# A hybrid encoder step: its input projection computed by Strassen's seven products

## What is computed

```python
h = rmsnorm(x, norm_g)
proj = jnp.einsum('btd,de->bte', h, w_in)      # (tokens, 1024) x (1024, 3592)
pu, pg, q, k, v, ag, fl, cb, cc, cx, cgate = jnp.split(proj, _split_points(), axis=-1)
# pool branch: trailing means of pu minus pu, times pool_w, gated by silu(pg)
q = rmsnorm(q.reshape(B, T, N_ATT_HEADS, HEAD_DIM), q_norm_g)
k = rmsnorm(k.reshape(B, T, N_ATT_HEADS, HEAD_DIM), k_norm_g)
logf = jax.nn.log_sigmoid(fl + b_f)            # forgetting attention over q, k, v, logf, gated by silu(ag)
z = cc * cx                                    # conv branch: cb * causal conv of width 3 of z, gated by silu(cgate)
x_out = x + jnp.einsum('bte,ed->btd', mixed, w_out)
```

## Time and profile before

| | us |
|---|---|
| median of 3 runs | 1608.34 |
| lowest and highest | 1605.97, 1609.19 |
| the profiled execution | 1604.41 |
| its span | 1602.6 |
| first product of the input projection | 18.32 |
| prompt attention's first transposes | 747.13 |

### The profile page before, as it was taken

One profiled execution on the slowest core, in us unless ns is written; L12 is line 12 of the kernel. 1 busy time (PEld: TensorE's weight loads), 2 busy tenths in 40 slices (PEclk: granted clock), 3 DMA queues, 4 the chain that ended last, 5 costly groups with the idle time before them and its releaser, 6 DMA issues.

```text
span 1602.6 us, 24609 instructions
## 1 busy us (share of the span) xinstructions
PE 1536.1 (96%) x9264; PEld 1355.1 (85%) x9264; DVE 821.8 (51%) x2069; ACT 631.3 (39%) x1347; POOL 410.6 (26%) x706
## 2 busy tenths in 40 slices
PE   6999999999999899999999999999998999899999
PEld 5998888878799899898888888888887778688887
DVE  3333112232444422214988988888896788832221
ACT  4443121121211201113877877877975444410100
POOL 1110005555400000022444444444423355200000
PEclk9999999999999899999999999999999999899999
DMA  5433122121110200422133233233233665634441
GB/s 150 149 108 100 42 87 76 47 92 53 62 51 20 70 19 11 85 44 49 36 76 64 58 69 71 49 67 72 49 116 113 222 217 184 238 109 141 129 148 66
DMA packets 181511, 144.63 MB, mean 90 GB/s; under 512 B 104016, under 2 KB 140785, under 8 KB 181393
## 3 DMA queue, kind: packets, MB, share of 16 engines
q1 hardware_dynamic: 178880, 134.08, 28.8%
q10 hardware_dynamic: 2448, 8.91, 1.4%
q0 software_dynamic: 64, 0.07, 0.1%
HBM read 106.50 MB, written 36.53 MB: 89 GB/s over the span
## 4 chain that ended last, share of the span: by engine, by line
PE 52%; DVE 6%; ACT 4%; DMA 2%; issue 2%; POOL 1%; SPq 0%; ACTq 0%; POOLq 0%
PE banks L2263 12%; PE banks L920 12%; PE banks L1546 6%; PE banks L1537 4%; PE banks L1532 3%; PE banks L1562 3%; PE banks L1563 3%; DVE sa_v_lo L1920 2%; PE banks L2021 2%; PE banks L2002 2%; PE banks L1515 2%; ACT pa_s_ring L1386 1%; ACT pa_pt_hi L1415 1%; DMA pa_q_raw<-scratch_q 1%; PE banks L2051 1%
## 5 line engine op out<-in xcount | busy, mean ns | idle before, releaser
L914 PE MATMUL banks<-in_w_hi,in_xt_hi 128*128 128x512 f32 (+1 forms) x680 | 242.4, 356 | 4.6 <-DVE in_w_lo L644 3.1
L914 PE MATMUL banks<-in_w_hi,in_xt_lo 128*128 128x512 f32 (+1 forms) x680 | 239.6, 352 | 0.0
L914 PE MATMUL banks<-in_w_lo,in_xt_hi 128*128 128x512 f32 (+1 forms) x680 | 238.7, 351 | 0.0
L1436 DVE CUSTOM_DVE_ANT_0 pa_s_ring<-banks,pa_f_b 128x512 f32<-128x512 f32 (+2 forms) x320 | 193.2, 604 | 35.8 <-PE banks L1537 33.1
L920 PE MATMUL banks<-in_xt_hi,in_w_hi 128*128 128x384 f32 (+1 forms) x576 | 196.7, 342 | 8.2 <-DVE in_w_lo L644 8.0
L1484 DVE TENSOR_TENSOR pa_pt_lo<-banks,pa_pt_hi 128x512 fp32r<-128x512 f32 (+2 forms) x320 | 193.0, 606 | 21.3 <-ACT pa_pt_hi L1415 18.7
L920 PE MATMUL banks<-in_xt_hi,in_w_lo 128*128 128x384 f32 (+1 forms) x576 | 191.9, 333 | 0.0
L920 PE MATMUL banks<-in_xt_lo,in_w_hi 128*128 128x384 f32 (+1 forms) x576 | 191.8, 333 | 0.0
L1415 ACT ACTIVATE pa_pt_hi<-banks 128x512 fp32r<-128x512 f32 (+2 forms) x320 | 166.6, 534 | 54.1 <-PE banks L1546 52.9
L1546 PE MATMUL banks<-ident,pa_s_ring 128*128 128x128 f32 x1088 | 174.0, 275 | 9.7 <-DVE pa_pt_lo L1484 4.2
L1562 PE MATMUL banks<-pa_pt_hi,pa_vs 128*128 128x256 f32 x576 | 163.6, 300 | 0.4 <-DVE pa_parts L1464 0.3
(11 more groups left out here) (245 smaller groups left out, 2810.8 us busy)
## 6 DMA issues: line engine op xcount, KB each, us to landing
sa_k_c<-in_cache_k_dram SPq DMA_DIRECT2D x8, 2048.0 KB, 9.8
sa_v_c<-in_cache_v_dram SPq DMA_DIRECT2D x8, 2048.0 KB, 8.2
in_w_raw<-in_w_in_dram SPq DMA_DIRECT2D x48, 256.0 KB, 3.7
out_dram<-in_out SPq DMA_DIRECT2D x34, 256.0 KB, 2.0
out_dram<-op_y ACTq DMA_DIRECT2D x17, 512.0 KB, 5.1
in_x<-in_x_prompt_dram SPq DMA_DIRECT2D x16, 512.0 KB, 3.5
op_x<-in_x_prompt_dram SPq DMA_DIRECT2D x16, 512.0 KB, 4.9
pa_f_b<-scratch_f SPq DMA_DIRECT2D x28, 256.0 KB, 5.2
```

Of the source, the lines that this page charges most:

```text
L914: mm = pe.matmul(ps[:, u % NBANK, 0:n], tile_of(xa, t)[:, k, :], wa[:, k, c0:c0 + n], start=(k == 0 and q == 0), stop=(k == KT - 1 and q = ...
L1436: done = dve.tensor_tensor_reduce(scores_of(j)[:, b * P:(b + nb) * P], ps_s[:, (h * NQD + at) % 3, 0:nb * P], f_b[h % 2][:, b * P:(b + nb) ...
```

## The change

The input projection is computed by one level of Strassen's scheme in Winograd's form. Operand x is a pair of token tiles (A1., A2.) with the model's depth in halves (A.1, A.2); operand w has its depth in halves and each phase's columns in halves. Eight block products become seven, each of 4 k x 3 matmuls:

| no. | x operand | w operand |
|---|---|---|
| 0 | A11 | B11 |
| 1 | S2 = S1 - A11 | T2 = B22 - T1 |
| 2 | S1 = A21 + A22 | T1 = B12 - B11 |
| 3 | S3 = S2 - A22 | T3 = B12 - B22 |
| 4 | A12 | B21 |
| 5 | S4 = A12 - S2 | B22 |
| 6 | A22 | T4 = B21 - T2 |

The norm's gain goes to x, in one pass of DVE (SCALAR_TENSOR_TENSOR with g_b in SBUF), not to w. ACT copies product 0 out of PSUM (`copy_first`, L811); DVE adds product 1 (`make_u`, L1200), product 2 (`make_v`, L1206) and the rest to the four quarters (C22 L1221, C12 L1229, C21 L1257; C11 by ACT, L831 or L857, from bank 0, where product 4 is accumulated on product 0). Products 0 to 3 have a PSUM bank each, products 4, 5, 6 go to banks 0, 2, 3.

The 17 tiles go in three blocks: 3, 3 and 2 pairs, and the sample tile in the third, computed without Strassen from the same w operands (`sample`, L1569 and L1572, 48 matmuls a phase for rows). A "work" is one pair in one phase (channels: one of two column halves, over all tokens of a half block). ITEMS gives the order of phases; where one phase's block is followed by the same phase's, the weights stay. There are 19 sets ("gens") of weights. Each has a top and a bottom buffer (8 loads of 256 KB, for CONV0 and CONV1 16 of half that, issued when the former set's last low half is made), four sums T1 to T4 on POOL (`add_weights`, L609 to L617), seven high halves on ACT (L804) and seven low halves on DVE (L1033), all in single buffers. ACT may write the high half n when the last work of the former set has done product n, and product n of the first work waits for the low half n.

The x sums are DVE's (L1005 to L1026), their low halves POOL's (`split_sums`, L624), the other low halves DVE's (L984), the high ones ACT's (L791). Rows of KEY and QRY go to SBUF first: squares by ACT (L880), reduce by DVE (L1041), scale by POOL (`qk_scale`, L632 and L636), multiply by DVE (L1049), gain by DVE for the second tile (L1056) and by POOL for the first (L642). The pool branch and the convolution are in blocks of 768 or 512 tokens. Prompt attention waits for the same events under new names.

The core of the diff (by_rows and by_channels of before; of after the order, SP's load, POOL's steps, ACT's and DVE's, the product and PE's loop):

```diff
-def by_rows(u, t, k, c0, n):
-    for q, (xa, wa) in enumerate(((xt_hi, w_hi), (xt_hi, w_lo), (xt_lo, w_hi))):
-        mm = pe.matmul(ps[:, u % NBANK, 0:n], tile_of(xa, t)[:, k, :], wa[:, k, c0:c0 + n],
-                       start=(k == 0 and q == 0), stop=(k == KT - 1 and q == 2))
-    return mm
...
-def by_channels(u, c, k, c0):
-    for q, (wa, xa) in enumerate(((w_hi, xt_hi), (w_hi, xt_lo), (w_lo, xt_hi))):
-        mm = pe.matmul(ps[:, u % NBANK, 0:chunk_tokens(c)], wa[:, k, c0:c0 + P], xa[c][:, k, :],
-                       start=(k == 0 and q == 0), stop=(k == KT - 1 and q == 2))
-    return mm
...
+HALF = (3, 3, 2)
+BASE = (0, 6, 12)
+NBLK = 3
+ITEMS = ([(0, ph) for ph in (GATE, KEY, QRY, POOL, CONV0, CONV1, VAL)]
+         + [(1, ph) for ph in (VAL, KEY, QRY, POOL, CONV0, CONV1, GATE)]
+         + [(2, ph) for ph in (GATE, VAL, KEY, QRY, POOL, CONV0, CONV1)])
+A11_B11, S2_T2, S1_T1, S3_T3, A12_B21, S4_B22, A22_T4 = range(7)
+BANK = (0, 1, 2, 3, 0, 2, 3)
...
+def w_source(ph, n):
+    wd = width(ph)
+    return (quarter(ph, 0, 0), t2[:, :, 0:wd], t1[:, :, 0:wd], quarter(ph, 0, 1), quarter(ph, 1, 0),
+            quarter(ph, 1, 1), t4[:, :, 0:wd])[n]
...
+def load_w(gen):
+    ph = gens[gen]
+    if gen:
+        sp.wait_ge(w_lo_done, 7 * gen)
+    for top, dst, sem in ((0, w_top, top_in), (4, w_bot, bot_in)):
...
+def add_weights(gen, n):
+    ph = gens[gen]
+    wd = width(ph)
+    if n == 0:
+        pool.wait_ge(top_in, loaded(gen))
+        pool.wait_ge(bot_in, loaded(gen))
+        pool.tensor_tensor(t1[:, :, 0:wd], quarter(ph, 0, 1), quarter(ph, 0, 0), ALU.subtract).then_inc(t_made, 1)
+    elif n == 1:
+        pool.wait_ge(t_made, 4 * gen + 1)
+        pool.tensor_tensor(t2[:, :, 0:wd], quarter(ph, 1, 1), t1[:, :, 0:wd], ALU.subtract).then_inc(t_made, 1)
+    elif n == 2:
+        pool.tensor_tensor(quarter(ph, 0, 1), quarter(ph, 0, 1), quarter(ph, 1, 1), ALU.subtract).then_inc(t_made, 1)
+    else:
+        pool.wait_ge(t_made, 4 * gen + 2)
+        pool.tensor_tensor(t4[:, :, 0:wd], quarter(ph, 1, 0), t2[:, :, 0:wd], ALU.subtract).then_inc(t_made, 1)
+def split_sums(f):
+    b, i = FORMS[f]
+    dst = x_op[slot_of(b, i)]
+    for n, (op, tmp) in enumerate(((S1_T1, 0), (S4_B22, 2), (S3_T3, 1))):
+        pool.wait_ge(xh_done, before(f, 7, 3) + (4, 5, 7)[n])
+        pool.tensor_tensor(dst[:, op, 1, :, :].rearrange("p k n -> p (k n)"), s_tmp[tmp][:, :],
+                           dst[:, op, 0, :, :].rearrange("p k n -> p (k n)").bitcast(F32),
+                           ALU.subtract).then_inc(xs_done, 1)
+def qk_scale(w, a):
+    n = qk_count(w, a)
+    at = a
+    pool.wait_ge(qk_ss, n + 1)
+    pool.tensor_scalar(h_ms[:, at, :], h_ss[:, at, :], 1.0 / HD, EPS, ALU.mult, ALU.add).then_inc(qk_rs, 1)
+    pool.wait_ge(qk_rs, 2 * n + 1)
+    if qk_count(w, 0):
+        pool.wait_ge(qk_mul, qk_count(w, 0))
+    pool.tensor_tensor(h_rstd[:, at, :], h_ms[:, at, :], neg_half[:, :], ALU.pow).then_inc(qk_rs, 1)
...
+x_scale(0)
+x_scale(1)
+pool.memset(pw[:, :, :], 0.0).then_inc(made, 1)
+pool.wait_ge(t_made, 2)
+add_weights(0, 2)
+split_sums(0)
+add_weights(0, 3)
+x_scale(2)
+x_scale(3)
...
+if prev and prev.phase in (KEY, QRY):
+    for a in range(len(tiles(prev))):
+        qk_scale(prev, a)
+if w.phase in (KEY, QRY) and w.makes:
+    add_weights(w.gen + 1, 2)
+    add_weights(w.gen + 1, 3)
...
+if w.last and w.phase in (CONV0, CONV1):
+    mult_z(w.block, w.phase - CONV0)
+gen = w.gen + 1
+if ITEMS[w.item][1] != ITEMS[min(w.item + 1, len(ITEMS) - 1)][1]:
+    if w.index == 1:
+        add_weights(gen, 0)
+        add_weights(gen, 1)
+    if w.last and w.phase not in (KEY, QRY):
+        add_weights(gen, 2)
+        add_weights(gen, 3)
...
+def high_w(gen, n):
...
+if gen:
+    last = [w for w in works if w.gen == gen - 1][-1]
+    act.wait_ge(proj, done(last, n))
+act.activation(w_half(ph, n, 0), w_source(ph, n), ACT.Copy).then_inc(w_hi_done, 1)
...
+square_x(0)
+high_x(0, 0)
+square_x(1)
+keep_x(0)
+high_w(0, 0)
+for n in range(1, 7):
+    high_x(0, n)
+    high_w(0, n)
+square_x(2)
+square_x(3)
...
+if w.strassen:
+    copy_first(w)
+if here == (2, CONV1, 3):
+    after_work(1)
+if prev and prev.makes:
+    high_w(prev.gen + 1, 5)
+    high_w(prev.gen + 1, 6)
...
+if w.makes:
+    high_w(w.gen + 1, 0)
...
+if prev:
+    finish(prev)
+if w.makes:
+    high_w(w.gen + 1, 1)
+    high_w(w.gen + 1, 2)
...
+c11(w)
...
+if w.makes:
+    high_w(w.gen + 1, 3)
+    high_w(w.gen + 1, 4)
...
+def low_w(gen, n):
+    ph = gens[gen]
+    dve.wait_ge(w_hi_done, 7 * gen + n + 1)
+    dve.tensor_tensor(w_half(ph, n, 1), w_source(ph, n), w_half(ph, n, 0).bitcast(F32),
+                      ALU.subtract).then_inc(w_lo_done, 1)
...
+def make_u(w):
+    n = tokens(w.block) if w.phase >= POOL else width(w.phase)
+    dve.wait_ge(proj, done(w, S2_T2))
+    dve.wait_ge(s1_done, w.pairs + 1)
+    if w.pairs:
+        dve.wait_ge(c21_done, w.pairs)
+    dve.tensor_tensor(u2[:, 0:n], ps[:, 1, 0:n], sv[:, 0:n], ALU.add).then_inc(u_done, 1)
+def make_v(w):
+    n = tokens(w.block) if w.phase >= POOL else width(w.phase)
+    dve.wait_ge(proj, done(w, S1_T1))
+    dve.wait_ge(u_done, w.pairs + 1)
+    dve.tensor_tensor(sv[:, 0:n], ps[:, 2, 0:n], u2[:, 0:n], ALU.add).then_inc(v_done, 1)
...
+def product(w, n):
+    b, ph = w.block, w.phase
+    if n == A11_B11 and w.n:
+        pe.wait_ge(c11_done, w.n)
+    elif n == S2_T2 and w.pairs:
+        pe.wait_ge(u_done, w.pairs)
+    elif n == S1_T1 and w.n:
+        pe.wait_ge(c12_done, w.n)
+    elif n == S3_T3 and w.pairs:
+        pe.wait_ge(c21_done, w.pairs)
+    elif n == A12_B21:
+        pe.wait_ge(s1_done, w.pairs + 1)
+    elif n == S4_B22:
+        pe.wait_ge(v_done, w.pairs + 1)
+    elif n == A22_T4:
+        pe.wait_ge(c22_done, w.pairs + 1)
+    if w.fresh:
+        pe.wait_ge(w_lo_done, 7 * w.gen + n + 1)
+    if ITEMS.index((b, ph)) == 7 * b:
+        wait_x(w, n)
+    for k in range(4):
+        for q, (xh, wh) in enumerate(((0, 0), (0, 1), (1, 0))):
+            opens, closes = OPENS[n] and k == 0 and q == 0, k == 3 and q == 2
+            if ph < POOL:
+                mm = pe.matmul(ps[:, BANK[n], 0:width(ph)], x_op[slot_of(b, w.at)][:, n, xh, k, :],
+                               w_op[n][:, wh, k, 0:width(ph)], start=opens, stop=closes,
+                               skip_group_check=not OPENS[n])
+            else:
...
+pe.wait_ge(made, 2)
+turn_x(0)
+for w in works:
+    aside(w, -1)
+    for n in range(7 if w.strassen else 2):
+        if w.strassen:
+            product(w, n)
+        else:
+            sample(w, n)
+        aside(w, n)
```

2071 lines of the change are left out of this document (1253 added, 818 removed).

## The result

The changed kernel takes **1711.8 us** (median of 4 runs, 1708.9 to 1714.7), the kernel before 1607.2 (1605.6 to 1609.2). The ratio is 1.0651, with a 95% interval of 1.0634 to 1.0669: slower by 105 us. Forecast were 1664 and a range of 1587 to 1710.

What follows compares the result with a forecast made beforehand. PE was taken to bound the input projection. From 1604.4 us: products -66.7, start +22.4, old gaps -25.2, switches +57, +40, +8, x +10, clock +10, sum +55.5, giving 1659.9; plus 3.9 for the median, 1664 (range 1587 to 1710).

Steps and rivals of the forecast that it cites:

- Start and gaps of before: Input projection: first product near 42.4 us, +22.4 us; the old kernel's idle and clock losses go, -25.2 us.
- Products: PE in the input projection: 4680 short matmuls become 3768 longer ones, priced by width, -66.7 us.
- Contention: Weight switches: DVE subtractions and POOL sums, both reading SBUF, run nearly one after the other, 2.5 to 4 us a switch.
- the walk: KEY to QRY switch followed through POOL's queue: T3, T4 and their halves late, about 7 us without contention.
- The clock: PE goes to half clock after waits at the 18 switches, 3.4 us lost each time, three times: +10 us.
- x formed beside products: Eight works that form x operands beside their products, some 10.5 us of DVE in 9.95: 1.2 each, +10 us.
- six out of KEY or QRY: Six weight switches out of KEY or QRY: late T3, T4 and halves plus contention, 9.5 us each, +57 us.
- eight out of POOL, CONV0, CONV1: Eight weight switches out of the channel phases: late loads and sums plus contention, 5 us each, +40 us.
- four others: Four switches between GATE, VAL and KEY, with no scales in POOL's queue: 2 us each, +8 us.
- The rival of the powers: POOL's 34 powers (1.64 us each) also block DVE: 42 us more, 1706; 0.16 together with the clock rival.
- The rival of the clock at every switch: PE's clock falls at each of 18 switches: 56 us in place of 10, 1710; 0.16 together with the powers.
- Faster: Switches nearly covered, stalls and clock in the stage under 69.5 us: mostly 1570 to 1601 us; chance 0.26.

Runs made afterwards that it cites:

- e9: Changed kernel with each POOL weight sum replaced by three fills that only write, about 2.45 us (values wrong): 1660.5 us, ratio 1.0332.
- e5: Changed kernel plus 24 unread 256-column matmuls put into PE's waits, twice at each of four switches (KEY to QRY, QRY to POOL, first two blocks): 1708.3 us, ratio 1.0632.
- e1: Changed kernel with all weight sets after the first left out (loads, sums, halves and the products' waits for them): 1568.2 us, ratio 0.9755.
- e8: Changed kernel with second pair's transposes behind product 3 of the first work, and DVE instead of POOL making T3, T4 at all 18 switches: 1661.6 us, ratio 1.0349.
- e11: As e8, and DVE also makes T1 and T2 where the next set is formed in GATE, VAL, KEY or QRY works: 1636.7 us, ratio 1.0192.
- e2: Changed kernel with POOL's four sums of every weight set after the first replaced by fills of 8 columns (values wrong): 1611.3 us, ratio 1.0028.
- e10: Changed kernel with all but 8 columns of DVE's seven low halves left out in every weight set after the first: 1647.7 us, ratio 1.0252.

## Why the prediction was wrong

**Its direction and its mechanism held, its size did not.** The range was missed by 1.8 us, the centre by 48.

- *Start and gaps of before*: right, 42.22 for 42.4. *Products*: 8.7 us too good by the price of N=128.
- *What ends the waits*: right as a chain, wrong as a label. The prediction said 100 us or more would be ended by L1033; it is 18 of 108, and DVE's additions end 66. L1033 at a mean of 1.5 to 1.8 us was right (1.64). The waits were said to be longest at products 3 to 6 after KEY and QRY; those at product 3 are there (3.79, 4.46 and 4.00 us), but the longest are 9.34 and 6.68, at product 5 of the last POOL work.
- *Contention*: right in mechanism and about right in size, 43 against e9's 51. One of its readings was off: by the rows shown, the four subtractions and the multiply, 4.1 us of work, took 3.77, not 3.94.
- **The step that failed is the cost of a switch: the walk, which gave no loss to the last work ahead of it, and "The clock": "three times, +10" beside it.** PE idles for 108 us against 115 forecast, but the lower clock takes 60 more. The two can't be added as separate prices, though. e5 shows it: with the clock up the waits grow. What was mis-sized is the time that DVE and POOL need for a switch, of which I had only counted how late one item comes for a PE at full speed. By the experiments' windows (first product to last):

| part | forecast | measured |
|---|---|---|
| price of N=128 | 0 | 9 |
| x formed beside products | 10 | e1, with its other short waits: 665.9 - 638.2 = 28 |
| switches without contention, clock in it | 42 + 12 + 8 + 10 = 72 | e9 - e1: 759.1 - 665.9 = 93 |
| contention | 43 | after - e9: 806.3 - 759.1 = 47 |
| together | 125 | 177 |

So up to 18 of the 52 us are in the forming of x, which I had priced by DVE's 10.5 us in a work of 9.95, without the norms ahead of the transposes: the transposes wait for them at 58.44 (5.11), 315.52, 333.39, 601.02 and more, 12.9 us after the start, and the clock falls behind. 21 are in the switches without contention. Where they are is told by the distances between the first products of the works, less the same work's in e1 (so waits and slow clock count alike):

| switches | forecast | e9 - e1: last work of the old set, first of the new | after - e9 |
|---|---|---|---|
| six out of KEY or QRY | 42 + 15 | 21.5 + 40.1 | 14.2 |
| eight out of POOL, CONV0, CONV1 | 12 + 28 | 18.8 + 2.6 | 25.9 |
| four others | 8 | 4.9 + 4.2 | 7.2 |
| the clock | 10 | in the rows above | |

For the first works of the new set the walk out of KEY and QRY came out right in size: 7 us each, measured 40.1 / 6 = 6.7, though 2.6 of that is slow clock and not waiting. What it had at nothing is the last KEY work, which it let run at full speed. There POOL reaches T1 and T2 only behind the scale and gain of the works before. DVE's second low half waits for T2 and ACT, and C22, behind it in DVE's queue, holds product 6. The last QRY work of block 0 begins at 152.0 (POOL and DVE of the kernel after; T2 is done at 164.56):

```profile
161.33 3.23 POOL L612 TENSOR_TENSOR in_t<-in_w_bot,in_t 128x1024 f32<-128x1024 f32 x1
...
165.69 1.23 DVE L1033 TENSOR_TENSOR in_w_op<-in_t,in_w_op 128x1024 fp32r<-128x1024 f32 x1 [3.02 <-ACT in_w_op L804]
```

Moving T1 and T2 is what tells: in e8 these six last works lose 37.5 us against e1, in e11, where DVE makes T1 and T2 in the phase's second work, 18.1. The port adds to it. In the switch from POOL to CONV0 the waits of 6.68 us at 206.55 and 9.34 at 477.95 (rows in e5), where 5 for the whole switch were forecast, are 1.72 and 2.97 in e9 (at 189.86 and 443.68), so there the port is most of it. Ahead of the first of them DVE's two pool sums of some 128x780 take 3.0 us each beside POOL's T2 and T3, and 0.97 in e9. What else holds the last works of the channel phases (18.8 us without contention) was not taken apart. The first of these waits in e9:

```profile
189.86 4.86 PE L1561 MATMUL banks<-in_x_ops,in_w_op 128*128 128x384 f32 x24 [1.72 <-DVE in_sv L1218]
```

- *The rival of the powers* is refuted. In the kernel after a DVE scaling with both inputs in SBUF starts and ends inside a power of POOL (L636) in 0.68 us (two more, at 381.04 and 677.30, take 0.71 and 0.68), and beside POOL's multiply by the gain (L642) the same scaling takes 1.79 (timeline):

```profile
109.85 1.65 POOL L636 TENSOR_TENSOR in_h_rstd<-in_h_ms,in_neg_half 128x8 f32<-128x8 f32 x1
111.47 1.30 POOL L642 TENSOR_TENSOR in_out<-in_out,in_qk_g 128x512 f32<-128x512 f32 x1
...
110.38 0.68 DVE L1049 TENSOR_TENSOR in_out<-in_out,in_h_rstd 128x512 f32<-128x512 f32 x1
111.54 1.79 DVE L1049 TENSOR_TENSOR in_out<-in_out,in_h_rstd 128x512 f32<-128x512 f32 x1 [0.48 <-POOL in_h_rstd L636]
```

The Trainium skill, "SBUF — State Buffer", section "Who interferes with whom", has one lock for the whole instruction in both cases. It fits the sums, behind which a subtraction ends 1.1 us late, about its own length, and the gain. It doesn't fit the powers, which read SBUF and hold up no DVE instruction for 1.64 us: there the measurement decides. How a power reads SBUF no row shows.
- *The rival of the clock at every switch* named 1710, and in size it fits: 56 us for the clock, where 60 were measured. But e5 takes away the reason: the half clock is there, and it isn't what the time is made of at the four switches tried. That its number came out is no proof of it.
- *Faster*: its condition, stalls and clock under 69.5 us, is missed by a factor of 2.5. Even with POOL's sums almost gone (e2) the time is 0.3% over that of the kernel before.
- *Later stages*: 5.6 us that I had carried over unchanged. The prompt attention begins with a wait of 3.34 us at 854.02 for ACT (L2030), where before it was 1.05 at 751.65; the clock falls to 0.93 from 848.5 to 900. ACT waits there for DVE, which first adds the last part of the convolution (L1155, 1.65 us at 850.74, itself 1.75 behind POOL). The weight sets are not the cause: e1 has the same wait, 3.36 us at 713.67.

## What to carry to other kernels

An algorithm that saves PE's time and gives it to the vector engines has to be priced by these engines' total per period, with the time that they exclude each other, and not by how late the worst item comes. Here 58 us of products were saved, and each of 18 switches brought 4 x 2.39 + 7 x 1.22 = 18 us of weight work for POOL and DVE beside works of 10 to 15 us. Where DVE and GpSimd both read two operands from SBUF, count their times as one sum; moving GpSimd's sums to DVE, at half the time each, gained 78 us. When such a period is walked through, start one work ahead of it, with what each queue still holds.
At a switch that the vector engines bound, an idle PE and a slow PE are two faces of one wait: filling the gaps with matmuls raised the clock and left the time as it was.

## What the runs showed of the hardware

- A POOL fill of 128x1024 (0.95 us) beside DVE's subtractions leaves these at 1.22 us; a POOL sum of the same area makes them 2.3 to 3.1. So here POOL's reading is what excludes; its writing alone does not.
- Both sides lose: T1, T2 and T4 take 2.67, 2.84 and 2.94 us on the mean, and 2.60, 2.47 and 2.50 with DVE's low halves almost gone (e10).
- A power on POOL (1.64 us for 8 elements) did not lengthen a DVE scaling with both inputs in SBUF: 0.68 to 0.71 us in three cases inside a power, 1.77 to 1.79 beside POOL's multiply.
- Products of 128 columns follow each other at 0.111 us, of 256 at 0.118: half the columns saved 6%.
- ACT's rounding of 128x1024 from SBUF took 1.05 us, less than the 1.15 taken from L1386.
